# Second mixer of a hybrid decoder layer: the transpose of a chunk's keys moved to the head of its step on the tensor engine

## What is computed

```python
s   = einsum('lk,sk->ls', q, k) * exp(log_d - m_row)      # scores within the chunk, gated
num = einsum('ls,sv->lv', s, v) + inter * einsum('vk,lk->lv', c_prev, q)
den = sum(s) + inter * einsum('k,lk->l', n_prev, q)
h   = num / maximum(abs(den), exp(-m_row))
c_new = s_prev * c_prev + s_loc * einsum('l,lv,lk->vk', wts, v, k)   # the state handed on
```

## Time and profile before

| | us |
|---|---|
| runs | 1071.98, 1074.06, 1075.29 (median 1074.06) |
| the profiled execution | 1072.99 |
| its span | 1071.3 |
| PE busy | 1053.1 (98%) |
| weight loads busy (beside PE) | 853.0 (80%) |
| DVE busy | 774.6 (72%) |
| GpSimd (POOL) busy | 687.8 (64%) |
| ACT busy | 539.8 (50%) |

### The profile page before, as it was taken

One profiled execution on the slowest core, in us unless ns is written; L12 is line 12 of the kernel. 1 busy time (PEld: TensorE's weight loads), 2 busy tenths in 40 slices (PEclk: granted clock), 3 DMA queues, 4 the chain that ended last, 5 costly groups with the idle time before them and its releaser, 6 DMA issues.

```text
span 1071.3 us, 18681 instructions
## 1 busy us (share of the span) xinstructions
PE 1053.1 (98%) x6343; PEld 853.0 (80%) x6343; DVE 774.6 (72%) x1186; ACT 539.8 (50%) x1286; POOL 687.8 (64%) x469
## 2 busy tenths in 40 slices
PE   7999999999999999999999999999999899999997
PEld 6887887877877888888878888888777788788886
DVE  5964785776866967776776686769588647766897
ACT  7544755746646643554445454545466345113543
POOL 3577555556555569668966797569859984635441
PEclk9999999999999999999999999999999999999999
DMA  6225132132151232224313433232329439676424
GB/s 221 71 93 90 41 119 80 41 119 74 44 158 49 80 118 80 83 56 137 119 51 92 126 92 94 88 117 89 102 94 376 137 118 330 205 275 260 166 99 137
DMA packets 122078, 131.79 MB, mean 123 GB/s; under 512 B 7884, under 2 KB 97288, under 8 KB 120472
## 3 DMA queue, kind: packets, MB, share of 16 engines
q1 hardware_dynamic: 107048, 84.42, 25.7%
q10 hardware_dynamic: 14960, 46.47, 12.7%
HBM read 96.16 MB, written 34.70 MB: 122 GB/s over the span
## 4 chain that ended last, share of the span: by engine, by line
PE 88%; POOL 3%; DVE 2%; DMA 2%; ACT 1%; DVEq 1%; POOLq 1%; issue 0%; ACTq 0%; SPq 0%
PE ps L1104 66%; PE ps L1407 5%; PE ps L1011 4%; PE ps L1221 3%; POOL ring_lo L836 2%; PE ps L1202 2%; PE ps L1276 2%; PE ps L1348 1%; POOL t L831 1%; PE ps L1330 1%; PE ps L1345 1%; DVE u_m L2704 1%; PE ps L1342 1%; PE ps L1296 1%; PE ps L1363 1%; DMA ev<-gm_scratch 1%
## 5 line engine op out<-in xcount | busy, mean ns | idle before, releaser
L836 POOL TENSOR_TENSOR ring_lo<-w,ring_hi 128x512 fp32r<-128x512 f32 x144 | 213.3, 1503 | 86.8 <-ACT ring_hi L1539 86.8
L836 POOL TENSOR_TENSOR ring_lo<-t,ring_hi 128x512 fp32r<-128x512 f32 x108 | 152.2, 1414 | 141.3 <-ACT ring_hi L1539 141.3
L1104 PE MATMUL ps<-s_hi,ring_hi 128*128 128x512 f32 x576 | 228.7, 397 | 1.8 <-issue 1.8
L1104 PE MATMUL ps<-s_lo,ring_hi 128*128 128x512 f32 x576 | 225.1, 391 | 0.0
L1104 PE MATMUL ps<-s_hi,ring_lo 128*128 128x512 f32 x576 | 225.0, 391 | 0.0
L1104 PE MATMUL ps<-h_hi,ring_hi 128*128 128x512 f32 x432 | 170.7, 395 | 2.6 <-POOL ring_lo L836 1.4
L1104 PE MATMUL ps<-h_lo,ring_hi 128*128 128x512 f32 x432 | 169.0, 391 | 0.0
L1104 PE MATMUL ps<-h_hi,ring_lo 128*128 128x512 f32 x432 | 168.6, 390 | 0.0
L1539 ACT ACTIVATE ring_hi<-w 128x512 fp32r<-128x512 f32 x144 | 86.7, 623 | 110.4 <-PE ps L1104 93.7
L1104 PEld LDWEIGHTS ps<-s_hi,ring_hi 128*128 128x128 f32 x576 | 108.2, 188 | 26.0 <-issue 5.1
L1104 PEld LDWEIGHTS ps<-s_hi,ring_lo 128*128 128x128 f32 x576 | 108.2, 188 | 22.4
(11 more groups left out here) (317 smaller groups left out, 2072.0 us busy)
## 6 DMA issues: line engine op xcount, KB each, us to landing
w<-in_w_in SPq DMA_DIRECT2D x128, 256.0 KB, 2.9
xs<-in_x SPq DMA_DIRECT2D x8, 512.0 KB, 8.2
ga_scratch<-ev ACTq DMA_DIRECT2D x4, 1024.0 KB, 4.1
u_scratch<-silu_z ACTq DMA_DIRECT2D x8, 512.0 KB, 3.2
c_rows<-c_scratch ACTq DMA_DIRECT2D x8, 512.0 KB, 6.7
ev<-u_scratch SPq DMA_DIRECT2D x8, 512.0 KB, 4.6
u_sums_scratch<-ev ACTq DMA_DIRECT2D x4, 1024.0 KB, 5.0
gm_scratch<-ev ACTq DMA_DIRECT2D x4, 1024.0 KB, 5.1
```

Of the source, the lines that this page charges most:

```text
L836: return nc.gpsimd.tensor_tensor(flat(lo[:]), flat(raw_or_sum[:]), flat(hi[:]).bitcast(F32), ALU.subtract)
L1104: mm = nc.tensor.matmul(ps[:, bank, columns], w[:, k, :], h[:, k, columns], start=(m == 0), stop=(m == PRODUCT - 1))
```

## The change

In each step with c below 8 the transpose of the chunk's keys is issued directly behind the waits and the increment of `passed`, ahead of the quarter products. `m_scores`, which the transpose incremented, is now incremented by the last score matmul. Source, destination and operation of the transpose are the same.

```diff
@@ -1321,6 +1321,8 @@
                         if m > 1:
                             pe.wait_ge(m_inter, 7 * p + m - 1)
                     pe.sem_inc(passed, 1)
+                    if c < NB:
+                        nc.tensor.transpose(ps[:, X[1], P:2 * P], mk_T[:, c * P:(c + 1) * P], ident[:])
                     if c:
                         if m:
                             for half in range(2):
@@ -1339,10 +1341,9 @@
                             for j in range(2):
                                 rows, out = slice(64 * j, 64 * j + 64), slice(64 * half, 64 * half + 64)
                                 keys = slice(c * P + 64 * half, c * P + 64 * half + 64)
-                                nc.tensor.matmul(ps[out, X[j], 0:P], mk_T[rows, keys], mq_T[rows, c * P:(c + 1) * P],
-                                                 start=True, stop=True)
-                        tok = slice(c * P, (c + 1) * P)
-                        nc.tensor.transpose(ps[:, X[1], P:2 * P], mk_T[:, tok], ident[:]).then_inc(m_scores, 1)
+                                mm = nc.tensor.matmul(ps[out, X[j], 0:P], mk_T[rows, keys], mq_T[rows, c * P:(c + 1) * P],
+                                                      start=True, stop=True)
+                        mm.then_inc(m_scores, 1)
                     if c:
                         for j in range(2):
                             mm = nc.tensor.matmul(ps[:, X[2], j * (MV + 1):(j + 1) * (MV + 1)], dmat[:, j, :], v1[:, m, j, :],
```

## The result

In eleven executions each, alternating, the changed kernel took 1077.61 us (median; 1074.57 to 1080.16) and the kernel before 1074.58 us (1071.98 to 1075.76). The ratio is 1.0029, 95% interval 1.0018 to 1.0039. One execution of the changed kernel in the second measurement (1505.48 us, at a mean granted clock of 0.655) and one of the kernel before in a later one (2708.47 us) were far slower than all the others, and the ratios leave them out.

A forecast was written before the change was run, and what follows sets the result against it. PE's own stream was taken to bound the kernel (busy 98% of the span); 32 steps at +0.05 us gave +1.6 us on the median 1074.06, so 1075.7 us (+0.15%), range 1072.8 to 1078.8 us.

The forecast's parts named there:

- PE alone sets the time of the stretch: 418 to 797 us: PE busy 379.00 of 379.00 us, so a microsecond of its stream is a microsecond of time.
- (a): Chunks 1 to 7, last product matmul to turning at the step's head: 0.23 us, the other bound being 0.32 us.
- slower rival: Waits and increment keep the turning's load from early fetching: 0.32 us ahead of it, +0.14 us a step, 1078.6 us; chance 0.13.
- (b): Chunks 1 to 7, turning to first quarter product: 0.20 us, a turning's slot of 0.11 and the crossing of 0.09.
- (c): Chunks 1 to 7, quarter products (scores) to values: 0.33 us, as scores to turning took before.
- (d): Chunks 1 to 7, values to next product: 0.47 us instead of 0.36, as the turning no longer covers dmat's load.
- The rival by which the load is fetched during quarter products: dmat's load stays covered, values to product 0.36 us, 1.9 us won, 1072.2 us; chance 0.11, half-way case included.
- The sum: Whole kernel: 32 changed steps at +0.05 us each, +1.6 us of PE.
- m_scores buys nothing: m_scores comes some 0.2 us earlier in its step without gain, since DVE first waits for the same step's values.
- no new wait: PE's queue in the last head pair has 1.3 us of slack, ten times the delay, so no wait is added.
- The delay reaches the end: Behind the last turned step, PE's delay passes through ACT to POOL, and all that follows moves 1.6 us later.
- swallowed rival: POOL and the weights' DMA of 797 to 847 us don't move; the 4.45 us absorb the delay: 1074.1 us; chance 0.08.

The follow-up runs named there:

- second measurement: The changed kernel run again with no edit, against the kernel before: 1074.83 against 1072.91 us, ratio 1.0012, interval 0.9999 to 1.0025.
- turned twice: Against the kernel before, keys turned both at the head of the step and between scores and values: 1077.26 us, ratio 1.0034.
- turned last: Against the kernel before, values issued ahead of the turning, so they open behind the quarter products: 1074.70 us, ratio 1.0009.
- values in front: Against the kernel before, chunks 1 to 7 issue the values at the head and the turning behind the scores: 1073.55 us, ratio 1.0003.
- turned inside: Against the kernel before, the turning stands between state products and scores: 1083.70 us (5 executions), ratio 1.0095.
- not turned: Changed kernel without turning the keys of chunks 1 to 7, weighted keys made from chunk 0's: 1075.00 against 1074.00 us for the kernel before, ratio 1.0008.
- in quarters: Against the kernel before, the turning is done behind the scores by four quarter products with the identity: 1077.19 us, ratio 1.0027.

## Why the prediction was right, step by step

- *PE alone sets the time of the stretch*: right. It is full in both profiles, and the trace's sums and the medians agree (1.94 and 1.92 us in the repetition).
- *(a) product to turning 0.23 us, not 0.32*: right, 0.230 to 0.232 us in all 28 steps. The slower rival rested on waits and increment keeping the turning's load back; the load starts at 433.51, 0.23 us before the turning itself. What costs 0.09 us is the crossing.
- *(b), (c)*: 0.20 and 0.33 us, right.
- *(d) the values' load loses its cover*: right in size (0.468 us), and shown as the cause: turned twice brings 0.36 us back, turned last loses it with nothing at the head, values in front keeps the old time. The rival by which the load is fetched during quarter products falls in every one of these kernels: the load of the opener starts within 0.01 us of the opener itself. How much an opener pays goes with its load. A quarter product's load takes 0.13 us and 0.05 us of it shows, the turning's 0.14 and 0.06, the values' 0.19 and 0.10, and that of a product matmul as the opener (chunk 0 of the changed kernel) 0.19 and 0.11: in each case the load less some 0.08 us. No run changed the length of a load alone, so this price is read from four kinds of opener and not tested. The rule of the Trainium skill on loads pulled ahead (TensorE: Matmul & The Clock Gate, Step-by-step: what each phase is for) holds between full matmuls here (0.23 us ahead for the turning's load behind a product), and not across a crossing.
- *The sum*: 32 x 0.05 = 1.6 us; the steps cost 1.54 us. Missing was a term: I took the products behind a step as unchanged, and they cost another 0.40 us. Together 1.94 us. The time alone would not have told forecast and slower rival apart: 3.03 us between the medians of the first measurement lies midway between their 1.6 and 4.5 us. The gaps in the trace decided, and the rest of the 3.03 us is scatter that the prediction allowed for only in its range.
- *m_scores buys nothing, no new wait*: right. PE is busy for 379.00 of 379.00 us from 418 to 797 us.
- *The delay reaches the end*: right within 0.3 us. POOL's low part behind the last step came at 797.82 instead of 795.62 us, again after a wait for ACT (4.65 us instead of 4.56), and only 0.26 us went into PE's idle time. The swallowed rival falls.

```profile
797.82 1.31 POOL L836 TENSOR_TENSOR ring_lo<-t,ring_hi 128x512 fp32r<-128x512 f32 x1 [4.65 <-ACT ring_hi L1540]
```

## What to carry to other kernels

A small full-array matmul between quarter-array products and larger full ones is not in the way: it is the opener, and the one with the cheapest weight load should have that place, since whatever opens behind a crossing shows its load (0.06 us for the transpose, 0.10 for the float32 values). Moving it to where its own load is hidden only hands the exposure to the next. Count crossings first (0.09 us into quarter products; 0.11 us out of them, 0.33 against 0.22 us; the turning between quarter products cost 0.42 us, and that is its slot of 0.11, these two and the exposed loads of 0.06 and 0.05), then ask what opens behind each, and price an order by the distance between starts over the whole step; the duration of the one line that was moved tells the opposite story.

## What I had not expected of the hardware

**Product matmuls run slow for a while behind a step, by an amount that depends on the order in it.** Undisturbed ones start 226.7 ns apart (mean). The eleven gaps behind the first take 2493 ns at that rate. Behind the 24 steps with all parts they take 2514 ns in the kernel before and 2512 in the two others where turning and values stand together behind the quarters (turned twice, turned last), but 2529 in the changed one and 2533 to 2537 ns with values in front, turned inside, not turned, and in quarters, as behind every chunk 8 (2534). Single gaps lie between 224 and 236 ns, and all are back at 227 behind six gaps in the first group and behind nine in the others. In the four steps of chunk 1 the grouping is less clean: 2498 ns before, 2503 changed, 2522 turned last. No experiment tells why; in the one stretch compared, from 441 to 450 us, DVE and ACT do the same work at the same distances before and after.

**PE's clock can fall behind its idle time, and the executions scatter with late weights and with the clock.** In the profiled execution of values in front, PE waited 2.48 us for POOL and then ran at the lower level, 1.2 GHz, up to 845.35 us: its matmuls start 0.43 us apart instead of 0.23.

```profile
839.33 0.39 PE L1104 MATMUL ps<-s_hi,ring_lo 128*128 128x512 f32 x1
842.20 0.80 PE L1104 MATMUL ps<-h_hi,ring_hi 128*128 128x512 f32 x1 [2.48 <-POOL ring_lo L836]
842.79 0.63 PE L1104 MATMUL ps<-h_lo,ring_hi 128*128 128x512 f32 x1
843.22 0.63 PE L1104 MATMUL ps<-h_hi,ring_lo 128*128 128x512 f32 x1
...
845.35 0.40 PE L1104 MATMUL ps<-h_lo,ring_hi 128*128 128x512 f32 x1
845.58 0.39 PE L1104 MATMUL ps<-h_hi,ring_lo 128*128 128x512 f32 x1
```

That execution took 1076.22 us at a mean clock of 0.997, seven of the same kernel's eight at 0.998 or above 1072.9 to 1073.6 (median 1073.35). Of the 2.9 us between, 1.24 us are idle time of PE from 820 to 853 us (5.69 us instead of 4.45), and some 1.5 us are the seven slow matmuls, by an estimate from the distances of their starts. The idle time came first: POOL, for which PE waited, had itself waited 2.3 us for branch weights (`in_w_branch_attn`), where it waits 0.4 to 1.2 us in the eight profiles that are neither this one nor the one in quarters. The latter shows that late weights do not always bring the clock down: PE waited 3.58 us at 824 us there, and its clock stayed at the upper level.

In the nine other profiles the clock is at the upper level from 5 to 8 us up to the last 2 to 5 us of the span, so a mean of 0.998 or 0.999 holds no drop in between. Outside the quarters, where 0.997 and 0.998 took the same, every execution at 0.997 or less was slower than its kernel's median at 0.998 and above. That such a drop, and the longer wait ahead of it, lie behind those too is likely; this one profile alone shows it. How often such means came differed (10 of 12 executions of the quarters, 2 of 11 of the repeated change, 6 of 11 of the same change before), and whether a kernel's order has a part in that is open. The idle time at 820 to 847 us, where PE waits for POOL, may thus cost more than its 4.45 us.
